# Split products of a chunk interleaved over its two or four PSUM banks

## What is computed

```
h = rms_norm(x, norm_g) * (1.0 + scale) + shift
proj = h @ w_in
(hg_q, hg_f, hg_i, hg_g, at_q, at_k, at_v, at_g,
 ix_q, ix_k, ix_w, s5_u, s5_g, merge_g) = split_cols(proj)
ya = hgrn2_mixer(hg_q, hg_f, hg_i, lb, hg_onorm_g) * jax.nn.silu(hg_g)
yb = dsa_mixer(at_q, at_k, at_v, ix_q, ix_k, ix_w, positions, at_qnorm_g, at_knorm_g) * jax.nn.silu(at_g)
yc = s5_mixer(...) * jax.nn.silu(s5_g)
yd = jnp.einsum('bsnw,nwd->bsnd', jnp.stack([ya, yb, yc], axis=2), w_branch)
merged = jnp.einsum('bsnd,bsnd->bsd', jax.nn.sigmoid(merge_g).reshape(B, S, N_BRANCH, D), yd)
return x + gate * (merged @ w_out)
```

## Time and profile before

| | |
|---|---|
| time, median of 3 runs | 1265.19 us (1260.91, 1265.19, 1266.45) |
| span of the profiled execution (its own whole time is not listed beside it) | 1255.9 us |
| PE busy | 1225.1 us, 98% |
| PE weight loads busy | 990.3 us, 79% |
| DVE, ACT, POOL busy | 879.0, 507.2, 485.8 us (70, 40, 39%) |
| mean granted TensorE clock | 0.994 |
| DMA | 142 MB, mean 113 GB/s |

### The profile page before, as it was taken

One profiled execution on the slowest core, in us unless ns is written; L12 is line 12 of the kernel. 1 busy time (PEld: TensorE's weight loads), 2 busy tenths in 40 slices (PEclk: granted clock), 3 DMA queues, 4 the chain that ended last, 5 costly groups with the idle time before them and its releaser, 6 DMA issues.

```text
span 1255.9 us, 16148 instructions
## 1 busy us (share of the span) xinstructions
PE 1225.1 (98%) x6074; PEld 990.3 (79%) x6074; DVE 879.0 (70%) x1415; ACT 507.2 (40%) x840; POOL 485.8 (39%) x336
## 2 busy tenths in 40 slices
PE   7999999999999999999979999999999999999998
PEld 4787788887788788888848777888777788888886
DVE  5787777867387776986577487778655887677252
ACT  4454224753443343333243632266443344333331
POOL 0143433243463235555405333423435443245551
PEclk9999999999999999999979999999999999999999
DMA  9532211132322435464434212212323322465322
GB/s 360 199 134 68 60 59 54 64 116 70 102 66 77 130 86 204 165 234 141 162 100 166 86 52 64 71 34 74 129 67 92 102 60 86 116 232 194 98 83 67
DMA packets 63437, 142.01 MB, mean 113 GB/s; under 512 B 29440, under 2 KB 31616, under 8 KB 62592
## 3 DMA queue, kind: packets, MB, share of 16 engines
q1 hardware_dynamic: 54016, 137.84, 32.9%
q10 hardware_dynamic: 9344, 3.15, 1.0%
HBM read 128.12 MB, written 10.49 MB: 110 GB/s over the span
## 4 chain that ended last, share of the span: by engine, by line
PE 94%; DMA 1%; DVE 1%; SPq 1%; ACT 1%; issue 1%; POOL 0%; ACTq 0%; DVEq 0%
PE bank L1672 25%; PE bank L1674 24%; PE bank L1673 24%; PE bank L1852 4%; PE bank L1808 2%; PE bank L1818 1%; PE bank L1832 1%; PE bank L1906 1%; DMA arena<-in_wada 1%; PE bank L1921 1%; PE bank L1939 1%; PE bank L1940 1%; PE bank L1825 1%; PE bank L1926 1%; PE bank L1896 1%
## 5 line engine op out<-in xcount | busy, mean ns | idle before, releaser
L726 POOL TENSOR_TENSOR w_lo<-raw,w_hi 128x512 fp32r<-128x512 f32 (+1 forms) x166 | 236.8, 1426 | 748.6 <-ACT w_hi L760 748.5
L1672 PE MATMUL bank<-h_hi,w_hi 128*128 128x512 f32 x896 | 361.7, 404 | 3.8 <-ACT arena L837 1.6
L1674 PE MATMUL bank<-h_hi,w_lo 128*128 128x512 f32 x896 | 349.3, 390 | 0.0
L1673 PE MATMUL bank<-h_lo,w_hi 128*128 128x512 f32 x896 | 348.9, 389 | 0.0
L760 ACT ACTIVATE w_hi<-raw 128x1024 fp32r<-128x1024 f32 (+2 forms) x170 | 178.8, 1055 | 226.9 <-PE bank L1674 199.7
L727 POOL TENSOR_TENSOR w_lo<-raw,w_hi 128x512 fp32r<-128x512 f32 (+2 forms) x166 | 256.4, 1545 | 0.0
L1672 PEld LDWEIGHTS bank<-h_hi,w_hi 128*128 128x128 f32 x896 | 168.3, 188 | 48.2 <-issue 12.3
L1673 PEld LDWEIGHTS bank<-h_lo,w_hi 128*128 128x128 f32 x896 | 168.4, 188 | 38.5 <-issue 5.0
L1674 PEld LDWEIGHTS bank<-h_hi,w_lo 128*128 128x128 f32 x896 | 168.2, 188 | 35.7
L1672 PE MATMUL bank<-w_hi,h_hi 128*128 128x512 f32 (+1 forms) x256 | 97.8, 382 | 5.4 <-issue 3.6
L1673 PE MATMUL bank<-w_lo,h_hi 128*128 128x512 f32 (+1 forms) x256 | 95.7, 374 | 0.0
(11 more groups left out here) (282 smaller groups left out, 1830.2 us busy)
## 6 DMA issues: line engine op xcount, KB each, us to landing
raw<-in_wfull SPq DMA_DIRECT2D x170, 512.0 KB, 3.6
arena<-in_wada SPq DMA_DIRECT2D x48, 512.0 KB, 4.7
x_scratch<-xm SPq DMA_DIRECT2D x2, 2048.0 KB, 8.8
arena<-x_scratch SPq DMA_DIRECT2D x2, 2048.0 KB, 9.1
arena<-in_x SPq DMA_DIRECT2D x4, 512.0 KB, 6.6
arena<-in_s5m SPq DMA_DIRECT2D x2, 1024.0 KB, 5.6
u_scratch<-arena ACTq DMA_DIRECT2D x4, 512.0 KB, 4.5
arena<-u_scratch SPq DMA_DIRECT2D x8, 256.0 KB, 3.8
```

The lines of the kernel that those rows point to most:

```text
L726: nc.gpsimd.tensor_tensor(lo[:, :half], raw_chunk(n)[:, :half], hi[:, :half].bitcast(F32), ALU.subtract)
L1672: mm(out_, a_hi, b_hi, start=first, stop=False)
L1673: mm(out_, a_hi, b_lo, start=False, stop=False)
L1674: return mm(out_, a_lo, b_hi, start=False, stop=last)
```

## The change

The helper takes lists of banks and operands and goes round over the banks, one part of the split (n = 0, 1, 2) at a time. Both loops are turned inside out: k tiles outside, banks inside. All `wait_free` calls of a group now stand ahead of its first product. The number of matmuls, their shapes and what they add up stay as they are; the order in which products are added into a bank is the same.

```diff
-            def three(out_, a_hi, a_lo, b_hi, b_lo, first, last):
-
-                mm(out_, a_hi, b_hi, start=first, stop=False)
-                mm(out_, a_hi, b_lo, start=False, stop=False)
-                return mm(out_, a_lo, b_hi, start=False, stop=last)
+            def three(outs, pairs, first, last):
+
+                for n in range(3):
+                    for out_, (a_hi, a_lo, b_hi, b_lo) in zip(outs, pairs):
+                        ins = mm(out_, a_lo if n == 2 else a_hi, b_lo if n == 1 else b_hi,
+                                 start=first and n == 0, stop=last and n == 2)
+                return ins
...
-                    for t in range(NT):
-                        dst = wait_free(pe, (key, t)) if k0 == 0 else bank[t]
-                        ts = slice(t * P, (t + 1) * P)
-                        for kk in range(CHUNK_K[n]):
-                            k = k0 + kk
-                            last = three(dst[:, 0:width], h_hi[:, k, ts], h_lo[:, k, ts], wh[:, kk], wl[:, kk],
-                                         k == 0, k == ND - 1)
+                    dst = [wait_free(pe, (key, t)) if k0 == 0 else bank[t] for t in range(NT)]
+                    for kk in range(CHUNK_K[n]):
+                        k = k0 + kk
+                        tokens = [slice(t * P, (t + 1) * P) for t in range(NT)]
+                        last = three([d[:, 0:width] for d in dst],
+                                     [(h_hi[:, k, ts], h_lo[:, k, ts], wh[:, kk], wl[:, kk]) for ts in tokens],
+                                     k == 0, k == ND - 1)
...
-                    for ct in range(2):
-                        dst = wait_free(pe, (key, ct)) if kh == 0 else bank[BANKS.uses[(key, ct)][0]]
-                        for kk in range(KC):
-                            k = KC * kh + kk
-                            if name == "wo":
-                                pe.wait_ge(m_done, ND * l + k + 1)
...
+                    dst = [wait_free(pe, (key, ct)) if kh == 0 else bank[BANKS.uses[(key, ct)][0]] for ct in range(2)]
+                    x_hi, x_lo = (y_hi, y_lo) if halves == 1 else (h_hi, h_lo)
+                    for kk in range(KC):
+                        k = KC * kh + kk
+                        if name == "wo":
+                            pe.wait_ge(m_done, ND * l + k + 1)
+                        cols = [slice(ct * P, (ct + 1) * P) for ct in range(2)]
+                        last = three([d[:] for d in dst],
+                                     [(wh[:, kk, c], wl[:, kk, c], x_hi[:, k], x_lo[:, k]) for c in cols],
+                                     k == 0, kh == halves - 1 and kk == KC - 1)
```

## The result

The changed kernel takes 1276.84 us in the median (4 runs, 1275.3 to 1280.92), the kernel before in the same comparison 1265.49 us (4 runs). The ratio is 1.0105, with a 95% interval of 1.0078 to 1.0133: about 1% slower, 11.4 us between the medians. The same two kernels compared again beside more runs gave 1274.74 against 1262.24 us, ratio 1.0090 (1.0062 to 1.0118). The forecast was 9.2 us and 1274.4. In these comparisons the time of a run is about 2 us longer than its span; the 9.3 us between the median and the profiled span of the kernel before are thus mostly the difference between a median execution and the fast one that was profiled, and not, as the prediction has it, what lies around the span.

What follows compares the result with a forecast made beforehand. PE was taken as the bound, with 94% of the chain of waits. Rotation at 0 ns and later group starts of 9.2 us, added to the median of 1265.2, gave 1274.4 us; range 1266 to 1281 us.

Steps and rivals of the forecast that it cites:

- Rotation at 0 ns: In PE's stream, neighbouring products writing different banks cost and gain 0 ns each; products stay 227 ns apart.
- Rivals 2 and 4: PE's stream: 2, rotation pays, 1220 us (chance 0.05); 4, rotation itself upsets the stream, 1368 us or more (chance 0.02).
- 13 ns: Part of each PE product that does not grow with its columns; rotation could at most remove it, 54 us.
- The waits: First products of kvi, hf, q and hg, both layers, come 1.47, 0.77, 0.71 and 1.52 us later, waiting for the last bank.
- The term for iq in layer 0: At iq's start in layer 0, the first product waits for ACT's copies and comes 0.22 us later.
- the waits for DVE: PE's waits for lines 1309 (5.2 us) and 1208 (3.8 us): none counted back, at most 9.0 us.
- rival 1: At PE's waits for DVE or smaller ones, the added delays are hidden or made good: 1265 to 1271 us, chance 0.22.
- The sum: The added waits at group starts over both layers, 8.94 + 0.22 = 9.2 us.
- rival 3: Clock falls after PE's idles before hg and kvi: 1.7 us each, 6.8 us more after all four, 1281 us; chance 0.06.

Runs made afterwards that it cites:

- the waits alone: The kernel before, products in the old order, with all waits for a group's banks put ahead of its first product: 1273.75 us against 1262.21, ratio 1.0090.
- Sooner reading on the changed kernel: The changed kernel with ScalarE copying all kvi and q banks first, then squaring from the copy: 1263.69 us against 1262.21 of the kernel before, ratio 1.0014.
- the fillers: The changed kernel with products that add nothing to the output put into PE's waits before kvi, hf and hg: 1268.48 us against 1262.21 of the kernel before.

## Why the prediction was right

**Rotation at 0 ns.** Shown. The evidence was thin, above all two changes of bank among thirteen steps of the earlier trace rows, and a kernel with nearly every product rotated repeats its 227 ns. Rivals 2 and 4 are out: no 13 ns were to be had, and each low stretch of the clock, but for one at the very end behind PE's last matmul, begins during an idle of PE of 0.6 us or more or at most about 3 us behind its end, in all nine profiles (their clock is recorded from some 10 us on); none begins in the middle of the rotated stream. The Trainium skill ("TensorE: Matmul & The Clock Gate", "A second HAM failure mode: psum-queue depth-cycling") tells of a kernel that cycles through banks and whose clock swings because PE idles briefly between groups. The traces agree on the idles; that another bank at every product does it by itself is not borne out where the stream goes on without gaps: 1262.26 us rotated, 1262.21 not. What the 13 ns are stays open.

**The waits.** The terms hold to 0.01 us each (table above). The term for iq in layer 0, 0.22 us, shows as a wait of 0.15 us for line 778 with the waits alone and in the second profile of the changed kernel, and not at all in the first. It moves nothing that can be told: with the waits alone iq starts at 26.86 us, where it started at 26.93 before. Next to nothing was taken back by the waits for DVE. The one for line 1208 is 3.8 us before and after. The one for line 1309 did shrink to 2.2 us in the first profile, which the prediction had named as a sign of rival 1; but it is 5.1 and 5.4 in the other two profiles with these waits, and from the last product of layer 0 to iq's first in layer 1 it is 19.0 us before and 18.6, 18.9 and 18.9 in the three, so at most 0.4 us came back. Rival 1 is out.

**The sum.** 9.2 us were forecast, 11.4 and 12.5 measured. That 1274.4 us stands 0.3 us from the second median is luck: the time of the kernel before was taken from three runs and lies 3 us above its later medians, and that made up for a sum 3 us too small. The rest is for the most part rival 3, to which I gave a chance of 0.06 and a price of 1.7 us for each fall; by the prediction's own list, a granted clock under 1.00 at these starts was a sign of being wrong. So its account of the waits was right and its account of the clock was not. The price fits: hg's first twelve products took 1.4 us longer, and the whole fall 1.6. The chance was wrong: behind hg's 2.3 us the clock fell in both layers in each of the three profiles with these waits, behind kvi's in layer 0 in two of the three and in layer 1 in none, behind hf's in none. I had weighed it by one place in the kernel before, where PE had little to do for some time, and had not asked what such an idle looks like when it stands in the middle of dense work.

A rough split of the waits' cost: each run lists its mean clock, so what the low clock costs at most is span x (1 - clock). Before: 1262.8 - 1261 x 0.0096 = 1250.7 us in the mean of 24 runs. Waits alone: 1273.6 - 1272 x 0.0110 = 1259.6. Of 10.8 us between the means, 8.9 are left when the clock's part is taken off, which is the sum of the table, and 1.9 are clock. The clock's part is a difference from what the kernel before loses too, 12.1 us at most in the mean of its runs. Sooner reading on the changed kernel gives 1264.3 - 1262 x 0.0080 = 1254.2, 3.5 over before, where 8.9 - 5.2 = 3.7 should be. With the fillers it is 1268.2 - 1266 x 0.0077 = 1258.5, 7.8 over before, though its starts are 8.9 us late; that 1.1 us is open, near what the three decimals of the clock allow.

## What to carry to other kernels

- Before reordering a stream to avoid a suspected conflict, look for the places where it already does what the change would do everywhere. One distance between starts at such a place decides more than any rule.
- Interleaving over several buffers makes the first instruction wait for the last buffer. Count the starts at which the readers of the last buffer are not done, and the time by which they are late; have the readers release all buffers before they do anything else.
- Two microseconds of idle in the middle of dense matmuls can cost more than two: look at the granted clock behind each, and in more than one profile, for the same idle is not followed by the same clock each time.

## What was not expected

- An idle of PE of 2.3 us in a dense stretch was followed by 3.4 us at half the clock in both layers before hg, but filled with products that add nothing the late starts cost 5.3 us less over the whole kernel. Idles of 1.83 us before hf had no such fall in the three profiles. The length of the idle does not decide it alone. An idle of 1.2 us near 440 us, with line 1208 of DVE as what ended it, stands in all nine profiles and was followed by a fall in one, an idle of 0.85 us near 1060 in all nine and by a fall in two; before the small matmuls near 480 us PE idled up to 1.33 us, and falls of 6.8 us came behind 0.63, 1.19 and 1.33 but not behind 1.00. What else decides stays open.
- The kernel's scatter follows its mean clock: the 24 runs of before go from 1257.71 us at 0.994 to 1267.85 us at 0.987, with the same program. A difference under 1% is better read from the distances in the traces than from a few times.
